# Diffusion trunk with PEER experts on one core: v rows gathered in blocks of 8 tokens by 16 slots and summed in four column groups, u products against rows held in PSUM, steps written out

## The reference

```
q = (xc @ w_q)                         # 8 heads, two halves of 128
s1, s2 = q[..., :128] . keys1, q[..., 128:] . keys2
v1, i1 = top_k(s1, 16); v2, i2 = top_k(s2, 16)
cand = v1[..., :, None] + v2[..., None, :]
sv, si = top_k(cand, 16)               # 16 experts for each token and head
idx = i1[si // 16] * 128 + i2[si % 16]
g = softmax(sv)
u = u_tab[idx]                         # 16384 rows of 1024 floats a layer
a = gelu(einsum('chkd,cd->chk', u, xc))
out = einsum('chk,chkd->cd', g * a, v_tab[idx])
```

## Time and profile before

| | |
|---|---|
| median of three runs | 2988.36 us |
| profiled execution: span (its own time is not shown apart from it) | 3175.8 us |
| GpSimd busy | 1709.2 us, 54% |
| TensorE matmul busy | 2281.8 us, 72% |
| VectorE busy | 1622.6 us, 51% |
| ScalarE busy | 608.3 us, 19% |
| moved by DMA | 918.09 MB, of which 805.40 MB by GpSimd's queue |
| layer 0 gathers | 297.5 to 2143.8 us of the span |
| layer 1 gathers | about 2324 to 3166 us |

### The profile page before, as it was taken

The page is one execution under the profiler, slowest core; times in us unless marked ns, Lnnn a source line. Parts: engine busy times, 40 slices in busy tenths (PEclk is TensorE's granted clock), DMA queues, the critical chain, the costliest instruction groups (busy, mean ns, idle before and its releaser), DMA issues.

```text
span 3175.8 us, 26554 instructions
## 1 busy us (share of the span) xinstructions
PE 2281.8 (72%) x7694; PEld 1174.7 (37%) x7694; DVE 1622.6 (51%) x3941; ACT 608.3 (19%) x1356; POOL 1709.2 (54%) x1642
## 2 busy tenths in 40 slices
PE   6989547767786687776767767687876765547767
PEld 4768212333352344332243322346762222212222
DVE  1245764555574555654446644434376445565433
ACT  2141111122211121111111211124211111111111
POOL 0000757646647656567655577540046776656774
PEclk8999879988899999899888899889988998879998
DMA  9523969968869988999979999970358998888996
GB/s 304 194 67 106 333 224 360 348 229 293 313 242 372 331 310 303 359 348 337 345 288 330 316 360 375 348 275 27 102 205 295 362 364 307 302 305 307 354 370 251
DMA packets 329368, 918.09 MB, mean 289 GB/s; under 512 B 27408, under 2 KB 131616, under 8 KB 329120
## 3 DMA queue, kind: packets, MB, share of 16 engines
q0 software_dynamic: 221184, 805.40, 68.6%
q1 hardware_dynamic: 108064, 111.24, 10.8%
HBM read 915.49 MB, written 1.05 MB: 289 GB/s over the span
## 4 chain that ended last, share of the span: by engine, by line
PE 29%; issue 16%; POOL 15%; DMA 14%; DVE 12%; another core or an unknown queue 10%; ACT 2%; SPq 0%; POOLq 0%; DVEq 0%; ACTq 0%
POOL RING L511 15%; PE acc L1086 14%; DMA RING<-in_p_v,IV 10%; PE wk L1147 4%; PE wk L1267 3%; PE wk L1280 2%; DMA WR<-in_ada_w 2%; DMA RING<-in_p_u,IU 2%; DVE TI L600 1%; ACT SCR L996 1%; DVE STM L772 1%; PE wk L1115 1%; PE wk L1076 1%; DVE RING L611 1%
## 5 line engine op out<-in xcount | busy, mean ns | idle before, releaser
L1086 PE MATMUL acc<-RING,DG 128*128 128x512 f32 x3072 | 1511.5, 633 | 623.4 <-DMA RING<-in_p_v,IV 325.1
L611 DVE SCALAR_TENSOR_TENSOR RING<-RING,H 128x1024 f32<-128x1024 f32 x768 | 922.3, 1224 | 767.7 <-DMA RING<-in_p_u,IU 724.0
L511 POOL DMA_INDIRECT RING<-in_p_u,IU x768 | 830.0, 1081 | 661.8 <-DVE RING L611 227.6
L1086 PEld LDWEIGHTS acc<-RING,DG 128*128 128x128 f32 x3072 | 570.4, 198 | 1552.5 <-issue 1155.8
L511 POOL DMA_INDIRECT RING<-in_p_v,IV x768 | 855.0, 1113 | 292.1 <-issue 203.7
L919 ACT ACTIVATE DG<-ident,WT 128x128 f32<-128x128 f32 x768 | 294.1, 399 | 1272.9 <-PE acc L1086 882.6
L508 POOL COPY IU<-IDX 128x16 uint32<-128x16 uint32 (+1 forms) x48 | 15.1, 314 | 488.2 <-DVE WG L874 488.0
L619 DVE TENSOR_TENSOR acc<-acc,BC 128x1024 f32<-128x1024 f32 x48 | 59.1, 1232 | 187.2 <-PE acc L1086 96.9
L1280 PE MATMUL wk<-HT,WR 128*128 128x256 f32 x576 | 132.5, 387 | 13.6 <-issue 11.8
L1147 PE MATMUL wk<-WR,HT 128*128 128x256 f32 x448 | 107.7, 397 | 34.2 <-ACT HT L947 20.3
L1280 PEld LDWEIGHTS wk<-HT,WR 128*128 128x128 f32 x576 | 110.8, 194 | 33.0 <-issue 16.4
(11 more groups left out here) (160 smaller groups left out, 1726.1 us busy)
## 6 DMA issues: line engine op xcount, KB each, us to landing
WR<-in_ada_w SPq DMA_DIRECT2D x34, 1024.0 KB
WR<-in_p_w_q SPq DMA_DIRECT2D x18, 1024.0 KB
RING<-in_ada_w SPq DMA_DIRECT2D x14, 1024.0 KB, 11.9
RING<-in_p_u,IU POOLq DMA_INDIRECT x768
RING<-in_p_v,IV POOLq DMA_INDIRECT x768
WR<-in_o_w_in SPq DMA_DIRECT2D x8, 1024.0 KB
RING<-in_p_w_q SPq DMA_DIRECT2D x6, 1024.0 KB, 11.2
WR<-in_e_w_in SPq DMA_DIRECT2D x5, 1024.0 KB
```

Of the source, the lines that this page charges most:

```text
L511: pool.indirect_dma_start(out=ring[:, n % NU, :], out_offset=None, in_=tables[table], in_offset=bass.IndirectOffsetOnAxis(ap=rows, axis=0) ...
L611: nc.vector.scalar_tensor_tensor(out=U[:, s % NU, :], in0=U[:, s % NU, :], scalar=1.0, in1=H[:, tile, :], op0=ALU.mult, op1=ALU.mult, accu ...
L1086: ins = nc.tensor.matmul(acc[:, par, hf * 512:hf * 512 + 512], DG[:, s % 4, :], V[:, s % NV, hf * 512:hf * 512 + 512], start=(s == 0), sto ...
```

## The change

1. **v rows in blocks.** A v gather no longer brings slot s for 128 tokens, but all 16 slots of 8 tokens (8 x 16 = 128 rows on 128 partitions). The row numbers have to be turned for that: after `topk`, DVE spreads them (`expand` to IE), PE multiplies twice by a selector (stage `ixT`, 128x16) and DVE copies the result to IDV. The weights of a chunk are spread the same way (WE), PE makes the 16 stationary blocks of 32 columns with one matmul of 128x512 (stage `weights`), ACT copies them to ST. The diagonals (768 on ACT) go.
2. **Four column groups.** The sum of a block is a matmul with 32 columns into its own 32 PSUM partitions, four blocks (groups) after one another. The sums of a step wait until all four of its blocks have landed.
3. **One accumulator.** A tile's 8 chunks are summed into `acc[:, 0]` and `update` runs once a tile, 6 times in place of 48.
4. **Token rows in PSUM.** `acc[:, 1]` holds a copy of `H[:, tile]` (stage `xin`, two ACT copies a tile), and the u products read it there.
5. **Steps written out.** No loops; a chunk is four steps of four slots, and the pieces of other work are put behind single steps (`choosing`, `spread`). `topk` is cut into three parts, one behind each of three steps. CTX attention goes by 2 units in place of 4.
6. **GpSimd.** No copies of row numbers (L508), no `gate` with its extra semaphore instruction, offsets straight from IDX and IDV.
7. Around it: the rotary uses one scratch tile, the pool weights lie on both halves of the partitions.

```diff
+def choosing(l):
+    f = {}
+    for t in TILES[l]:
+        for h, tile, q in ((1, t, 2), (3, t, 3), (5, t + 1, 0), (7, t + 1, 1)):
+            if tile in TILES[l]:
+                for part in range(3):
+                    f[t, h, part] = [("topk", l, tile, q, part)]
+                f[t, h, 3] = [("ixT", l, tile, q)]
+    return f
...
+def first_choices(l):
+    return [("score", l, LAT, (0, 1))] + [("topk", l, 0, 0, p) for p in range(3)] + \
+        [("bc", l, LAT, (G2,)), ("score", l, LAT, (2, 3)), ("score", l, LAT, (4,)), ("ixT", l, 0, 0)] + \
+        [("topk", l, 0, 1, p) for p in range(3)] + [("score", l, LAT, (5, 6, 7)), ("ixT", l, 0, 1)]
...
-        (1, "1"): [("bc", 0, CTX, (G1, SC2, SH2, G2)), ("topk", 0, 1, 2), ("topk", 0, 1, 3), ("out", 0, CTX)],
...
+    spread(f, (0, 6, 0), (0, 7, 3), [("att", 0, CTX, i, i + 2) for i in range(0, 12, 2)])
+    spread(f, (1, 0, 0), (1, 2, 3), [("bc", 0, CTX, (G1, SC2)), ("bc", 0, CTX, (SH2, G2)), ("out", 0, CTX), ("norm", 0, 2, CTX),
+                                     ("hT", 0, 2, CTX), ("rows", 0, CTX), ("score", 0, CTX, (0, 1)), ("score", 0, CTX, (2, 3))])
...
-            def gate(s, value):
-                pool.wait_ge(s, value)
-                pool.sem_inc(gate_sem, 1)
...
+            def gather_v(c, s):
+                if c > 0 or s >= NV:
+                    pool.wait_ge(vsum, c * TOPK + s - NV + 1)
+                col = (c % PH) * TOPK + s
+                gather("v", V, s, IDV[:, (c // PH) % 2, col:col + 1], v_in)
...
-                                                   in1=H[:, tile, :], op0=ALU.mult, op1=ALU.mult,
+                                                   in1=acc[:, 1, :], op0=ALU.mult, op1=ALU.mult,
...
+            def expand(out, rows, nh):
+                return nc.vector.tensor_tensor(out.rearrange("p h (j k) -> p h j k", j=8),
+                                               rows.unsqueeze(2).to_broadcast([P, nh, 8, TOPK]),
+                                               M8[:, :].unsqueeze(1).unsqueeze(3).to_broadcast([P, nh, 8, TOPK]), ALU.mult)
...
+            def vsums(c, q):
+                n, h = c // PH, c % PH
+                if q == 0:
+                    pe.wait_ge(*evac(("wT", c)))
+                if (h, q) == (0, 0) and n > 0:
+                    pe.wait_ge(updated, 2 * n)
+                for s in range(4 * q, 4 * q + 4):
+                    pe.wait_ge(v_in[s % NV], 16 * (2 * c + s // NV + 1))
+                for hf in range(2):
+                    for g in range(4):
+                        s = 4 * q + g
+                        ins = nc.tensor.matmul(acc[32 * g:32 * g + 32, 0, hf * 512:hf * 512 + 512], ST[:, c % 2, s, :],
+                                               V[:, s % NV, hf * 512:hf * 512 + 512],
+                                               start=((h, q) == (0, 0)), stop=((h, q) == (PH - 1, 3)))
+                        if hf == 1:
+                            ins.then_inc(vsum, 1)
```

More of the change, by code:

```diff
@@ new lines, in schedule @@
+    spread(f, (1, 4, 0), (1, 6, 3), [("score", 0, CTX, (4, 5)), ("score", 0, CTX, (6, 7))])
+    spread(f, (1, 6, 0), (2, 1, 0), [("ada", 1, k) for k in range(5)])
+    spread(f, (2, 2, 0), (2, 5, 3), [("norm", 1, 1, LAT), ("hT", 1, 1, LAT)] + [("in", 1, b, (LAT,)) for b in range(6)] +
+           [("ada", 1, 5), ("ada", 1, 6)])
+    spread(f, (2, 6, 0), (3, 4, 3), [("rope", 1, 0, "qk"), ("rope", 1, 1, "qk"), ("ada", 1, 7), ("ada", 1, 8), ("tqk", 1, LAT, "q"),
+                                     ("tqk", 1, LAT, "k"), ("ada", 1, 9), ("ada", 1, 10), ("ada", 1, 11), ("ada", 1, 12)])
@@ L108, in schedule @@
           ("bc", 1, LAT, (SC2, SH2)), ("rows", 1, LAT)]
[L109 to L115 removed]
+    s += first_choices(1)
+    s += gather_stages(1, choosing(1))
     return s + [("final",)]
@@ L180, in work_order @@
             w += [(s[:3] + (a, h), "act") for a, h in score_steps(s[3])]
+        elif k == "ixT":
+            w += [(s, "dve")]
+        elif k == "weights":
+            w += [(("wT", chunk0(s[1], s[2]) + s[3]), "act")]
     return w
@@ L372, in program @@
         scaled = Count(sem("scaled"), all_units)
-        topks = named("topk")
+        xin = Count(sem("xin"), named("xin"))
+        topks = [s[:4] for s in named("topk") if s[4] == 0]
         shifted = Count(sem("shifted"), topks)
@@ L515, in chunk @@
[L515 to L535 removed]
+                                        in_offset=bass.IndirectOffsetOnAxis(ap=rows, axis=0)).then_inc(slot_in[n % NU], 16)
@@ L537, in _, with turned @@
+            def turned(l, c):
+                tile, h = (c - chunk0(l, 0)) // PH, c % PH
+                pool.wait_ge(*evac(("ixT", l, tile, h // 2)))
             for s in SCHEDULE:
                 if s[0] == "experts":
-                    _, l, tile, part = s
-                    if part == "0":
-                        pool.wait_ge(chosen.sem, chosen.at("topk", l, tile, 0))
-                        chunk(l, tile, 0, 0, tile - 1, slice(7 * TOPK, 8 * TOPK), True)
-                    elif part == "loop":
-                        with pool.Fori(1, PH // 2 - 1) as p:
-                            gate(chosen.sem, chosen.at("topk", l, tile, 1) - 1 + p)
-                            chunk(l, tile, p, 0, tile, bass.ds((2 * p - 1) * TOPK, TOPK), False)
-                            chunk(l, tile, p, 1, tile, bass.ds(2 * p * TOPK, TOPK), False)
-                    else:
-                        h = int(part)
+                    _, l, tile, h, q = s
+                    c = chunk0(l, tile) + h
+                    if q == 0:
```

401 lines of the change are left out of this document (186 added, 215 removed).

## The result

| | before | after |
|---|---|---|
| median of the runs made side by side | 2990.15 us | 2761.84 us (2760.22 to 2762.97) |
| ratio | 1 | 0.9226 [0.9201, 0.9251] |
| span of the profiled execution | 3175.8 us; a second one, below, 2972.7 us | 2759.9 us |

The forecast was 2755 us, so the total is met. Its parts aren't, as will be seen: the time of an undisturbed chunk, forecast to stay, fell, and the pauses held less than was counted.

A forecast was written before the change was run, and what follows sets the result against it. DMA was taken to bound the gather stages, GpSimd close behind. Gain 313 - 50 - 32 = 231 us, taken straight off 2988.4, gave 2757, stated as 2755; its own range 2680 to 2830, overall 2640 to 2870.

The forecast's parts named there:

- pauses come back: Gather stages of both layers: 313 us of pauses recoverable, less 50 us for projection, slow-clock starts and tile borders.
- DMA at 0.98 stands in front, so I take 0: Product operand in PSUM: GpSimd's pace might fall from 1.40 to 1.24 us, but DMA bounds the chunk, so 0.
- What could come back at most: Gather stages: 224 us in layer 0 and 89 in layer 1 above undisturbed chunks and weight loads, together 313 us.
- I leave 18 us: CTX output projection, still one piece of 29.60 us with four weight blocks for three slots: 18 us not recovered.
- Start: 32 us: Start of each layer: row-number copy waits for an `ixT` behind the last scores, costing 13.8 + 18.3 = 32 us.
- 0 as well: v sums of a step waiting for all four blocks: 4 to 6 us left before the slot's reissue, so 0.
- rival D: v ring: batches of four starve it, 3 us lost in each of 192 steps, 3330 us in all; chance 0.08.
- Clock, 0: TensorE pieces starting at 1.2 GHz: 1 to 2 us each, mostly covered.
- Rival B: TensorE pieces stay at 1.2 GHz, output projection 59 us, score pairs 28 to 32: 90 us more, 2845; chance 0.10.
- A: Gather pace rises to 1.24 us, a chunk takes 40 to 42 us: 190 us more gain, 2570; chance 0.14.
- C: DMA rate has no room, a clean chunk costs 47 us: 70 us less gain, 2825; chance 0.06.
- E: New waits chain the engines, a step's wait replaces each pause: no gain, 2988 us; chance 0.05.

The follow-up runs named there:

- a_sbuf: The changed kernel with the second operand of the u products read from H in SBUF again, copies into PSUM kept: 2883.41 us, ratio 0.9638.
- a_vonly: The changed kernel with token row read from SBUF, choices whole and other work only at chunk ends: 3011.18 us, ratio 1.0066 to the kernel before.
- a_start: The changed kernel with a layer's second `ixT` moved from behind the last scores to behind step 3 of the first chunk: 2758.37 us, ratio 0.9225.
- a_slot: The changed kernel with v sums made slot by slot, each after its own block's landing: 2741.19 us, ratio 0.918 to the kernel before.
- b_unrolled: The kernel before with its loops over heads 2 to 5 written out and nothing else: 2991.75 us, ratio 0.999.

## Why the prediction was right in its sum and wrong in its parts

The forecast was 2755, the result 2761.84; the gain was forecast as 231 us and measured as 228.3. The sum was 313 - 50 - 32 with the pace at 0. What the runs put in its place:

| step of the forecast | forecast | measured |
|---|---|---|
| pauses come back (choices split, work spread) | 313 - 50 = 263 | 27.2 + 60.2 = 87 undone one by one; 3011.2 - 2883.4 = 128 undone on top of the SBUF operand |
| product operand in PSUM | 0 | 121.6 |
| start of a layer | -32 | -24.6 in the trace of after, -32.8 in those of `a_sbuf` and `a_vonly` |
| v side, column groups, written-out code | 0 | `a_vonly` 21 slower, start included; some 11 faster without it |

**The step that failed, first: "DMA at 0.98 stands in front, so I take 0".** I read a DMA share of 0.98 in the earlier trace rows as a DMA that can't go faster. The chunk went from 45 to 41 us at the same bytes, and the rate from 368 to 410 GB/s. GpSimd stood in front: 32 gathers x (mean 1.10 + 0.30) is 44.8 of the 45.5 us. I had this sum (1.40 against 1.42) and called it close behind. The share counts an engine as busy while a packet is under way, however long the packet takes: a 4 KB packet took 176 ns on average before, 166 in after, and the share of the quicker chunk is 1.03. So a share near 1 doesn't say that nothing more would fit.

The prediction had drawn from the Trainium skill ("SBUF — State Buffer", Who interferes with whom) that the move would do nothing, because the page infers that the writing of descriptors isn't hit by a VectorE operation with two SBUF inputs. `a_sbuf` is against that conclusion: 1.99 us in place of 0.94 beside such products, and 121.6 us at the end. It isn't against the page's rule itself, by which such an operation contends with a GpSimd instruction that reads SBUF: an indirect gather has its row numbers there. Whether GpSimd loses the time reading them or writing descriptors, no run here shows.

**The second: "What could come back at most", the 313 us.** It stood wholly on one profiled execution that was 187.4 us longer than the median. I took the difference off straight, on the argument that the pauses come from engine work which doesn't shrink. They did shrink: a choice from 23.7 to 15.7 us, the pauses over 10 us from 421 to 120.5 (many became shorter than 10), all waits on the rings from 494 to 345. So 149 of the 203 us between the two traces of before were such waits. I treated them as common to both kernels and counted them as gain too. By the second of the two measures in the table the pauses brought 128 where I had 263, 135 too much, and the operand 121.6 where I had 0. The sign that I had given, waits of GpSimd under 150 us together, failed too: they are 386. That the two errors are of one size is chance.

**"I leave 18 us" for the output projection.** The pause there was 27.57 us, above the 15 to 25 that I gave as a sign. Splitting the piece gave about 19 at the end, near the 18.

**Start: 32 us.** The price was sized from the last scores. With the operand in SBUF it is 32.8 in the traces (50.1 us a start in `a_vonly`), and in after 24.6, because the gathers that refill the ring behind the pause take 0.94 us each and not up to 1.99. The cause was half right: I named the `ixT` behind the last scores alone. `xin` on ScalarE behind the same scores holds the products equally, which `a_start` showed by doing nothing, and the first `ixT` holds the second choice by 9.6 us.

**"0 as well" for the wait of four blocks.** `a_slot` is 20.7 us faster. In after there are 15 waits of 4 to 8 us at v gathers behind TensorE, 77.8 us together, in `a_slot` 7 with 41.2; this is rival D in the small, 0.1 us a step and not 3. As the clock changed with it, 20.7 us is what both together brought, and not the price of the wait alone.

**Written-out code, 0:** confirmed by `b_unrolled` (0.999). **Product from PSUM costs VectorE nothing:** 1219 against 1224 ns. **v sums at 0.24 us:** 0.211, as a mean over both clocks., from which the 0.24 was worked out, stand in a stretch of granted clock 0.50 (46.03 to 47.96 us of the first trace), so the 0.22 above is their match. "Eight of a step 2 us" is a slip, since a step has 16 records: 3.50 us at the low clock. **Clock, 0:** the output projection took 28.64 us in after and 29.60 in the earlier trace rows, though the mean granted clock had fallen to 0.68 in the stage. While it ran the clock was 0.97:

```profile
741.00:769.00 28.00, 28.00 (x128) 24.49 (x127) 4.16 (x6) 1.88 (x2) 3.08 (x4) 0.97 0.73 257
```

Rival B had 59 us for it, at a clock that stays at 1.2 GHz. That settles B.

**The rivals.** A (the pace rises) is what happened: 41 us, in its range of 40 to 42. Its price of 190 us more was too high: the operand brought 121.6, and the 190 were added to gains that weren't there. C (no room in the DMA rate) is out: 410 GB/s. The Trainium skill ("SBUF — State Buffer", A bandwidth-pool intuition that's wrong (but worth ruling out)) gives about 358 GB/s for HBM to a core; this trace, with one core at work, is above it at 410 GB/s. D is out as a mechanism of its size. E is out for the kernel as a whole; the one place where the engines are chained, the start, is priced above.

**What stays open.** Why one execution of before had pauses over 10 us of 421 us where the second had 120.5; how the 40 us of interaction come about; and which of its two effects gives `a_slot` its 20.7 us.

## What to carry to other kernels

Before a profile is used for a sum, set its span against the runs: if it is 6% longer, ask which rows hold the 6%, because a gain read off those rows isn't there in the runs. A resource at a 0.98 share is not shown to be the bound while another engine's issue times add up to the same period; compute both periods, and ask what would slow the issuing engine (here a second SBUF operand on VectorE, cured by reading it from PSUM at no cost). A faster form of work that is off the path brings nothing by itself: the column groups more than halved TensorE's time for the v sums, and summing slot by slot, at twice the time, was 0.75% faster.

## What the runs showed of the hardware that I hadn't expected

- An indirect gather of 128 rows of 4 KB takes GpSimd 0.94 us when VectorE's products read one operand from PSUM, with 0.30 us to the next, and up to 1.99 us beside products with two SBUF operands. The means are 0.96 and 1.14 us (after, `a_sbuf`). Where no two products followed each other closely, a chunk took 40.9 us with two SBUF operands as well (`a_sbuf`).
- One core's gathers ran at 410 GB/s over a whole chunk.
- 32-column float32 matmuls over 512 columns cost 0.12 us a record in four column groups in turn at granted clock 1.00 (1.92 us for 16), and 0.475 one after another in one group at the same clock (1.90 us for 4): a factor of 4. Half of it went to the clock here: in the clean chunks of after 16 took 3.50 us, so that the mean over the kernel is 0.211 against 0.418 in `a_slot`.
- TensorE's granted clock is no measure of a kernel's speed here: after is 7.7% faster than before by the medians, at 0.721 against 0.926 in the second trace of before.
